# Where the gate and branch work of one token mixer runs beside the attention of the next

## The reference

```
h = rmsnorm(x) * (1 + sc1) + sh1
xa_q, xa_kv, xb, xc, xd, gates = split(h @ w_in)
y_a = mla_mixer(xa_q, xa_kv)            # 8 heads, low-rank q and kv
y_b = chunk_relbias_mixer(xb)           # 8 heads, learned relative bias
y_c = diff_mixer(xc)                    # 4 heads, two maps each: softmax(0) - lam * softmax(1), then rmsnorm
y_d = swa_sink_mixer(xd)                # 8 query heads, 2 kv heads, window 128, sinks
branch = einsum(stack(y_a..y_d), w_branch)
merged = sum(sigmoid(gates) * branch)   # over the four branches
x = x + g1 * (merged @ w_out)
x = x + g2 * (shared_expert(h2) + routed_experts(h2))   # 64 experts, top 6
```

## Time and profile before

| | us |
|---|---|
| median of 3 runs | 3025.38 |
| lowest and highest run | 3019.72, 3032.05 |
| profiled execution, span from first to last instruction | 3027.5 |
| PE, DVE, ACT, POOL busy | 2832.9, 2117.6, 1651.9, 690.0 |

### The profile page before, as it was taken

The page is one execution under the profiler, slowest core; times in us unless marked ns, Lnnn a source line. Parts: engine busy times, 40 slices in busy tenths (PEclk is TensorE's granted clock), DMA queues, the critical chain, the costliest instruction groups (busy, mean ns, idle before and its releaser), DMA issues. The chain is left out here.

```text
span 3027.5 us, 44165 instructions
## 1 busy us (share of the span) xinstructions
PE 2832.9 (94%) x14520; PEld 2263.1 (75%) x14520; DVE 2117.6 (70%) x3015; ACT 1651.9 (55%) x2612; POOL 690.0 (23%) x563
## 2 busy tenths in 40 slices
PE   5999999899899999999779999989998999999995
PEld 4677776677678888888666777866776888888884
DVE  5544456555589899999845444565546989999997
ACT  2342433432358788888534434244323778888883
POOL 0100000000145653333200000001001567533330
PEclk9999999999999999999889999999998999999997
DMA  7224342233569999999812243422334999999995
GB/s 234 79 75 148 118 134 96 74 120 133 208 239 359 354 364 373 366 373 364 309 57 80 87 153 111 153 70 90 124 120 189 349 355 353 364 381 368 369 353 228
DMA packets 124560, 671.52 MB, mean 222 GB/s; under 512 B 27628, under 2 KB 29036, under 8 KB 90444
## 3 DMA queue, kind: packets, MB, share of 16 engines
q1 hardware_dynamic: 91040, 605.91, 54.4%
q0 software_dynamic: 31424, 57.44, 5.7%
q10 hardware_dynamic: 1932, 6.16, 0.9%
HBM read 656.60 MB, written 55.28 MB: 235 GB/s over the span
## 5 line engine op out<-in xcount | busy, mean ns | idle before, releaser
L2158 DVE TENSOR_TENSOR ew_lo<-ew,e_hi 128x2048 fp32r<-128x2048 f32 x258 | 591.3, 2292 | 95.2 <-ACT e_hi L1954 95.2
L711 PE MATMUL bank<-h_hi,w_hi 128*128 128x512 f32 x1248 | 511.9, 410 | 35.1 <-DVE w_lo L645 16.5
L1954 ACT ACTIVATE e_hi<-ew 128x2048 fp32r<-128x2048 f32 x260 | 498.6, 1918 | 15.2 <-PE bank L2373 9.3
L711 PE MATMUL bank<-h_hi,w_lo 128*128 128x512 f32 x1248 | 504.3, 404 | 0.0
L711 PE MATMUL bank<-h_lo,w_hi 128*128 128x512 f32 x1248 | 502.0, 402 | 0.0
L645 DVE TENSOR_TENSOR w_lo<-raw,w_hi 128x1024 fp32r<-128x1024 f32 x198 | 242.1, 1223 | 301.1 <-ACT w_hi L637 300.6
L2373 PE MATMUL bank<-e_hi,x_hi 128*128 128x512 f32 x1040 | 418.2, 402 | 0.1
L2373 PE MATMUL bank<-ew_lo,x_hi 128*128 128x512 f32 x1040 | 408.5, 393 | 0.0
L2373 PE MATMUL bank<-e_hi,x_lo 128*128 128x512 f32 x1040 | 406.0, 390 | 0.0
L711 PEld LDWEIGHTS bank<-h_hi,w_hi 128*128 128x128 f32 x1248 | 240.1, 192 | 116.6 <-issue 44.2
L1842 POOL DMA_INDIRECT y_d<-y,idx x130 | 214.5, 1650 | 467.6 <-issue 401.0
(11 more groups left out here) (331 smaller groups left out, 5065.0 us busy)
## 6 DMA issues: line engine op xcount, KB each, us to landing
ew<-in_wexp SPq DMA_DIRECT2D x130, 2048.0 KB, 9.8
raw<-in_wmix SPq DMA_DIRECT2D x297, 512.0 KB, 3.5
ew<-in_wexp SPq DMA_DIRECT2D x130, 1024.0 KB, 10.2
ew<-y_d SPq DMA_DIRECT2D x8, 2048.0 KB, 11.7
ew<-y_d SPq DMA_DIRECT2D x8, 1024.0 KB, 7.8
ada0a<-in_ada SPq DMA_DIRECT2D x2, 2048.0 KB, 13.4
ada0b<-in_ada SPq DMA_DIRECT2D x2, 2048.0 KB, 22.2
h_d<-htok ACTq DMA_DIRECT2D x8, 512.0 KB, 10.8
```

What stands on the lines that cost most here:

```text
L711: ins = nc.tensor.matmul(out, lhs, rhs, start=start, stop=stop)
L1954: nc.scalar.activation(e_hi[h][:], up_part(ew, j, h), ACT.Copy).then_inc(whi_done, 1)
L2158: nc.vector.tensor_tensor(up_part(ew_lo, j, h), up_part(ew, j, h), e_hi[h][:].bitcast(F32), ALU.subtract).then_inc(wlo_done, 1)
```

## The change

Of gbB's 16 jobs the second half leaves the stretch after B's attention and is spread between the maps of C's attention, ahead of projD's jobs. The order of all jobs and tiles stays as it is. Since these jobs still read B's output in `o_hi` and `o_lo` while C's sets are made, C's sets get buffers of their own, `oC`: `oC_lo` where `o2_lo` was, `oC_hi` in the space of B's keys and values, behind D's. D's sets go to `o_hi` and `o_lo`. gbC's branch jobs read `oC`. The wait for gbB's last job moves from C's first set to D's first.

```diff
-        o2_hi = place("o2_hi", [P, 4, S], F32R, at=r0 + 24576)
-        o2_lo = place("o2_lo", [P, 4, S], F32R, at=r0 + 32768)
+        oC_hi = place("oC_hi", [P, 4, S], F32R, at=r1 + 14336)
+        oC_lo = place("oC_lo", [P, 4, S], F32R, at=r0 + 32768)
...
-            act = "o2" if j.act == "o" and j.arg // KD == 3 else j.act
+            act = "oC" if j.act == "o" and j.arg // KD == 2 else j.act
...
-            if br in "BC" and o % 4 == 0:
-                wait_chunk_full(act, jobs["gb" + "ABCD"[o // 4 - 1]][-1].c)
-            dst = (o2_hi if br == "D" else o_hi)[:, o % 4, :]
+            if br in "BD" and o % 4 == 0:
+                wait_chunk_full(act, jobs["gbA" if br == "B" else "gbB"][-1].c)
+            dst = (oC_hi if br == "C" else o_hi)[:, o % 4, :]
...
-            hi, lo = ((o2_hi, o2_lo) if br == "D" else (o_hi, o_lo))
+            hi, lo = ((oC_hi, oC_lo) if br == "C" else (o_hi, o_lo))
...
-        shares = {br: spread(jobs[FILL[br]], NGROUP + 1) for br in "ABCD"}
+        fill = {br: jobs[FILL[br]] for br in "ABCD"}
+        alone = {br: jobs["gb" + br] for br in "ABD"}
+        held = len(jobs["gbB"]) // 2
+        fill["C"] = alone["B"][held:] + fill["C"]
+        alone["B"] = alone["B"][:held]
+        shares = {br: spread(fill[br], NGROUP + 1) for br in "ABCD"}
...
-                            act_stream(act, events_of(whole(jobs["gb" + br])))
+                            act_stream(act, events_of(whole(alone[br])))
...
-                            dve_stream(dve, events_of(whole(jobs["gb" + br])))
+                            dve_stream(dve, events_of(whole(alone[br])))
...
-                            for j in jobs["gb" + br]:
+                            for j in alone[br]:
```

More of the change, by code:

```diff
@@ L283, in hybrid_trunk @@
         prC = pr + [place(f"pr{4 + i}", [P, S], at=t_end["tab3"] + 2048 * i) for i in range(2)]
-        assert t_end["pr5"] <= t_end["o2_hi"]
+        assert t_end["pr5"] <= r0 + 32768 and t_end["oC_hi"] <= t_end["vB"]
         qD = place("qD", [P, 4, S], at=r1)
@@ L287, in hybrid_trunk @@
         vD = place("vD", [P, TC, P], at=r1 + 12288)
+        assert t_end["vD"] <= r1 + 14336
         cursor[0] = both_end
@@ L648, in hybrid_trunk @@
         acts = {"h": (h_hi, h_lo), "cq": (cq_hi, cq_lo), "ckv": (ckv_hi, ckv_lo), "m": (h_hi, h_lo),
-                "s": (s_hi, s_lo), "o": (o_hi, o_lo), "o2": (o2_hi, o2_lo)}
+                "s": (s_hi, s_lo), "o": (o_hi, o_lo), "oC": (oC_hi, oC_lo)}
         made = {}
```

## The result

| | before | changed |
|---|---|---|
| median of runs, us | 3025.36 | 2993.97 |
| lowest and highest, us | 3019.72, 3032.05 | 2985.59, 2996.47 |
| profiled span, us | 3027.5 | 2992.6 |

The ratio of the changed kernel to the one before is 0.9886, with a 95% interval of 0.9870 to 0.9901: 34.5 us faster, by the interval 30 to 39. The forecast was 21 us and 3004, in a range of 2992 to 3016. The plain median, 2993.97, lies 2 us inside it, but the forecast gain of 21 us lies outside the interval of 30 to 39, and the changed kernel run once more gave a ratio of 0.9891. The direction was right, the size was not.

A forecast was written before the change was run, and what follows sets the result against it. PE was taken to bound the kernel (94% busy), losing time to gaps and slow clock in C's attention. Per layer 10.2 + 1.4 - 1.0 = 10.6 us, two layers 21.2: 3025.4 - 21.2 = 3004 us, range 2992 to 3016.

The forecast's parts named there:

- The start gap, the 0.27 and the 3.25: PE gaps at C's pipeline start (1.29 us) and in its tail, which fill cannot reach; forecast to stay.
- the set's normalisation gaps: C's transposes waiting for a finished set's normalisation, 5.9 us; all but the tail's 3.25 forecast to go.
- the sum's first term, the 10.2 us: PE's waits in C's stretch that filling can reach, 15.0 - 3.5 - 1.3 = 10.2 us a layer, forecast to go.
- The 1.0 us for new waits: Charge per layer for C's slots where moved evictions, reductions and splits make DVE hold PE up; bounds nothing to half of 10.2.
- the 6.7 us: DVE's chain in a C slot from fill's end to next bias pass: eviction, reduction, split, copy, combine, biases; against PE's 6.2.
- the first slow stretch: PE at 1.2 GHz in 480.6 to 483.9, following C's start gap; forecast to stay.
- The second one: PE at 1.2 GHz in 497.7 to 501.0, in C; forecast to go with its gaps, winning 1.4 us a layer.
- more comes back: Rival: in C the first slow stretch and half the long one around D's start go too; 15.2 a layer, 2995 us; chance 0.14.
- the slow stretch at D's start: PE at half clock for 10.2 us around D's start, following C's tail; forecast kept, half gone in the 2995 rival.
- DVE keeps half: Rival: half of C's 10.2 us and the second slow stretch stay; sign negmax waits of 5 us or more; 3015; chance 0.19.
- DVE sets the pace: Rival: every C slot becomes a serial chain of 7.6 us, 8.4 us a layer slower, 3042 us; chance 0.05.
- The rule of the Trainium skill: Judges PE's headroom by weight loads' busy share: C's stretch 106.5 us instead of 110.2, total 2997.

The follow-up runs named there:

- e1_none: Changed kernel's buffers and waits alone, with all 16 of gbB's jobs left after B's attention: ratio 0.9996 to the kernel before.
- the comparison at full clock above: Kernel before and changed kernel, each with a DVE sum behind C's bias passes; B's jobs and C's attention in layers without slow clock: 152.8 and 137.7 us.
- e5_twice_before: Kernel before with each of projD's six projections multiplied twice, 144 more products between C's maps: ratio 1.0117 to the kernel before.
- e12_changed: The changed kernel itself, run again beside the other experiments on the same chip: ratio 0.9891 to the kernel before.
- e9_start: Changed kernel with the first 8 products of each attention's first share issued ahead of the second group's scores: ratio 0.9841 to the kernel before.
- e10_both: Changed kernel with e9_start's early products and C's shares over 19 slots, filled with gbC's first two gates: ratio 0.9828 to the kernel before.
- e11_order: e10_both with D's projections reordered, kD ahead of vt and a gbC gate between vt and its turn: ratio 0.9830 to the kernel before.

## Why the prediction was wrong in size

**The place held, and so did the rough mechanism.** C's was the stretch with the idle time, moving half of the jobs covers its waits, and the buffers and moved waits cost nothing (e1_none, and the unchanged 100.5 us of D's attention). ACT loads no table between the jobs' tanh and C's squares in either trace. The start gap, the 0.27 and the 3.25 stayed, the set's normalisation gaps went, DVE's share in C came out at 69% (66% forecast).

**The step that failed is the sum's first term, the 10.2 us.** It took the idle column as the whole of PE's waiting, and so put the waits that lie under busy records at nothing, without a reason. The forecast of the idle time itself came true, about 6 us for C against 5.8 measured, while C's stretch, forecast at 108 to 112 us, took 103.8 and 105.1. Per layer, forecast against measured in layer 1: idle time 10.2 - 1.0 = 9.2 against 10.0 (the 0.6 in B's jobs went as well); clock 1.4 against some 2.6; waits under busy records nothing against 5.0. Together 10.6 against 17.6, and 16.3 in layer 2, where one slow stretch stayed. By the comparison at full clock above the covered waits are 4.4, the idle time 10.7. That these 5.0 us were waits of PE and not a cost of the old place is shown by e5_twice_before, where products alone covered 19.0 us in layer 2 without anything leaving B's stretch. How they are shared out among single instructions is shown for the scores only (2.1 us).

**The 1.0 us for new waits was right in size, its reasoning half, so that is in part luck.** One gap of 0.97 us is there; up to 1.0 more may lie under busy records. The forecast looked for it in slots with an eviction, a reduction and a split together. Ahead of 490.64 DVE has a split and then the low part of C's set, which the 6.7 us left out, and the eviction comes behind the bias passes. Of DVE's 6.7 us only what lies ahead of the bias passes counts; the evictions and reductions behind them are free until they delay the next slot's combine. The runs with more jobs moved show where that limit lies: the ninth to twelfth job together cost more than they cover.

**The clock.** I kept the first slow stretch because its gap stays. In layer 1 the gap of 1.29 us stayed and the stretch did not come, in layer 2 both came, and in e12_changed, the same kernel, both came in both layers (the two stretches then took 138.2 and 138.7 us). So keeping it was right in three of these four layers, and layer 1's 17.6 us has 1.3 us of luck in it; whether such a stretch comes is not a matter of the kernel's order alone. The second one went in all four, as counted; e1_none has it in another place, so which gaps it hangs on is not shown.

**The rivals.** The nearest in size was "more comes back" (2995). Its reason holds at most in part: the slow stretch at D's start is 10.2 us in layer 1 as before, but 6.6 in layer 2, and 6.7 and 6.8 in e12_changed; the first slow stretch went in one layer of these four. It leaves the waits under busy records out as the forecast does, so its nearness is luck for the most part. "DVE keeps half" and "DVE sets the pace" fell with the waits on negmax, 2.3 us. The rule of the Trainium skill (Perfetto Trace Analysis, Identifying the Most-Contended Engine), to judge PE's headroom by the busy share of weight loads instead of matmuls, came nearer than my sum: it gave 106.5 us for C's stretch, and 103.8 and 105.1 were measured. The trace agrees with it that the busy share of pipelined matmuls is a poor measure: that share was 90% before in the stretches of B's jobs and of C together, and the same instructions then did without 7.6 us of it. The nearness of the 106.5 is partly luck: it took 78.7 us of weight loads at a share of 74%, and the changed kernel has 75.3 us of them at 73%.

## What to carry to other kernels

Value a gap on a pipelined engine from start to start of its instructions, not by the idle column: compare the step of the same instructions where nothing waits, and compare the length of equal groups in different places. To find what a stretch of small dependent steps could hold, double some work in it that nobody needs and see how little it grows. Where a queue is shared by a chain and by fill, an added operation costs what its place says; try it ahead of and behind the link that the other engine waits for. And a pipeline's start is worth a few products of fill of its own: here four starts a layer were worth 14 us, some 40% of what the change gave.

## What the runs showed of the hardware that was not expected

The same gap does not always lower PE's clock. Behind the start gap of C (1.29 us in both layers of the changed kernel) the granted clock stayed at its full level in layer 1 and was at half, 1.2 GHz, for a stretch of 3.3 us in layer 2; A's attention took 166.6 us in layer 1 and 169.4 at a clock of 0.98 in layer 2, with the same gap of 1.8 us; in the kernel before it took 166.5 at 1.00 in both layers. Two layers of one run can so differ by 1 to 3 us in a stretch, and comparing them is a cheap way to the clock's price. With the start gaps filled (e9_start) A's, B's and C's stretches ran at 1.00 in both layers; that is one execution, and A's had done so before with its gap, so it does not show that filling them prevents the fall. The long stretch at half clock around D's start is another matter: 10.2 us in both layers before, 10.2 and 6.6 in the changed kernel, and none in either layer of e10_both and e11_order, where the wait of 3.25 us in C's tail and D's start gap are both filled.
